# Suffix sums of a stick-breaking attention: fp32 matmuls replaced by fp32r matmuls on a high and a low part

## The chip, the cores and the metric

One core of one Trainium2 chip runs the whole program in one launch. The metric is the device time of a launch in microseconds (us). Below, TensorE is PE, ScalarE is ACT, VectorE is DVE, GpSimd is POOL, and SP issues the DMAs.

## The reference

The reference is a two-part model on a sequence of 256 positions, 1024 wide, in fp32: a block with a retention layer and a stick-breaking layer, each between two gated feed-forward layers and followed by a gated projection, and then a short convolution and a block attention. The change touches only the stick-breaking attention, with 8 heads of 128:

```python
def block(args):
    q_blk, b = args
    qpos = b * SB_BLOCK + jnp.arange(SB_BLOCK)
    z = jnp.einsum('bhqd,bhkd->bhqk', q_blk, k) * scale
    mask = (kpos[None, :] < qpos[:, None])[None, None]
    log_one_minus = jnp.where(mask, jax.nn.log_sigmoid(-z), 0.0)
    rem = lax.cumsum(log_one_minus, axis=3, reverse=True) - log_one_minus
    a = jnp.where(mask, jnp.exp(jax.nn.log_sigmoid(z) + rem), 0.0)
    return jnp.einsum('bhqk,bhkd->bhqd', a, v)
```

Around it stand `proj = h @ w_in` (1024 by 3072) and `o @ w_out` (1024 by 1024).

## The kernel before, in words

**The weight stream.** All weights of the model pass through the same pipeline, in slots numbered through the whole program. A slot is 256 rows by 512 columns of a weight. SP loads it into one of 4 `raw` buffers; ACT rounds it to fp32r as `w_hi` (`split` on ACT, L961); DVE makes `w_lo`, the rest that the rounding left (`split` on DVE, L1354); PE forms each product as three fp32r matmuls of 512 columns (hi by hi, hi by lo, lo by hi, L492 to L494, `products`). `w_hi` and `w_lo` are rings of 8 slots. SP reloads a raw buffer once `w_lo` of the slot four before is made.

**Orders written out by hand.** Each engine runs one program, in order. `split_to(n)` on ACT or on DVE means: make the parts of all slots below n that are not yet made. An instruction placed behind `split_to(n)` waits for all of them; and a `w_lo` on DVE waits for the `w_hi` of the same slot on ACT. PE works through the phases: `sb_in` (the projection, slots s0 to s0+23, in 12 groups, two groups for 4 slots, 24 matmuls each) and `sb_out` (slots s0+24 to s0+31). Between groups stand hooks with the attention's own work: after group 5 `sb_z` of heads 0 to 3 (the scores), after group 6 `sb_rem` of heads 0 and 1, after group 7 `sb_rem` of heads 2 and 3 and then `sb_mix` of heads 0 and 1 (weights by values), after group 8 `sb_mix` of heads 2 and 3; heads 4 to 7 have `sb_z` after group 10, `sb_rem` after step 1 of `sb_out` and `sb_mix` after step 3.

**One head.** PE writes z into a bank `turn[k]`. ACT makes log(1 + exp(-|z|)) in three steps (`sb_log`, L1181 to L1185). DVE adds max(z, 0) (L1638) and multiplies by the negated causal mask (L1642): the result `loss` is 384 columns wide, the three causal 128 by 128 blocks side by side. `sb_rem` then adds to the scores, in the same bank, the suffix sums of `loss`, by matmuls with a triangle of ones, with a block of ones, and with the identity on a tile of -1e30 outside the mask. All four are fp32 matmuls, and the trace shows each as two PE instructions (x16 for 8 heads). ACT then takes the exponential (`sb_exp`, L1191), and PE multiplies by the values. `sb_rows(m)` on ACT (L1162) copies the sums of group m out.

**The order on ACT** in this stretch: rows 4, flat, rows 5, `sb_log` 0 and 1, `split_to(s0+20)`, `sb_log` 2 and 3, rows 6, `sb_exp` 0 and 1, rows 7, `split_to(s0+24)`, and so on. Rows 7 wait for the sums of group 7. **On DVE**: `split_to(s0+16)`, `sb_loss` 0 and 1, `split_to(s0+20)`, `sb_loss` 2 and 3, `split_to(s0+24)`, the low parts of y for heads 0 to 3, `split_to(s0+28)`, `sb_loss` 4 to 7, `split_to(s0+32)`.

Of the kernel before, what the change touches and what calls it, by code (L numbers as in the profile page):

```python
# [23 lines left out]
F32 = mybir.dt.float32  # L24
F32R = mybir.dt.float32r
I32 = mybir.dt.int32
ACT = mybir.ActivationFunctionType
ALU = mybir.AluOpType
AX_X = mybir.AxisListType.X

P = 128
SEQ = 256
# [29 lines left out]
SW_QK, SW_V, SW_QT, SW_KT, SW_HEAD = 0, 1024, 2048, 3072, 4096  # L62
SW_MASK, SW_NEG, SW_TRI, SW_ONES = 7168, 7552, 7936, 8064
# [148 lines left out]
def build(nc, x, p_in, positions, norm_gains, ffn_w_gate, ffn_w_up, ffn_w_down, ret_w_in, ret_gn_gain,  # L212
          ret_w_out, sb_w_in, sb_w_out, ple_w_gate, ple_w_proj, norm_g_2, conv_w_in_2, conv_w_2,
          conv_w_out_2, attn_w_in_2, q_norm_g_2, k_norm_g_2, attn_w_out_2, consts, out):
    with ExitStack() as ctx:
        def sb(name, shape, dt=F32):
            return ctx.enter_context(nc.sbuf_tensor(name, shape, dt))

        def sem(name):
            return ctx.enter_context(nc.semaphore(name))  # L220
# [7 lines left out]
        y_hi = sb("y_hi", [P, FC, SEQ], F32R)  # L228
        y_lo = sb("y_lo", [P, FC, SEQ], F32R)
# [7 lines left out]
        ident = sb("ident", [P, P])  # L237
# [4 lines left out]
        work = sb("work", [P, WORK])  # L242

        sums = [ctx.enter_context(nc.psum_tensor(f"sums{i}", [P, COLS], F32)) for i in range(BANKS)]
        turn = [ctx.enter_context(nc.psum_tensor(f"turn{i}", [P, COLS], F32)) for i in range(4)]
# [24 lines left out]
        gn_loaded, decay_loaded, mask_loaded = sem("gn_loaded"), sem("decay_loaded"), sem("mask_loaded")  # L270
# [12 lines left out]
        mx = {n: sem("mx_" + n) for n in (  # L283
            "roped", "rope_step", "turned", "flat", "scores", "weights", "mixed", "stats", "gn_r",
            "gn_step", "gate", "y", "y_step")}
        sbs = {n: sem("sb_" + n) for n in ("turned", "flat", "z", "log", "act_step", "dve_step", "loss", "rem", "a", "o")}
        cv = {n: sem("cv_" + n) for n in ("mul", "turned", "flat", "step", "y", "pad")}
        mb = {n: sem("mb_" + n) for n in (
            "sq", "sq_step", "r", "normed", "turned", "flat", "s", "t", "max", "negmax", "exp",
# [17 lines left out]
        def lin(value, step, j):  # L307

            return value if j is None else j * step + value

        def wait_slot_free(eng, n, j=None):

            if n >= RING:
                kind, value = RELEASE[n - RING]
                if kind == "used":
                    eng.wait_ge(slot_used, lin(value, 6, j))
                else:
                    eng.wait_ge(sums_done, lin(value, 4, j))

        def mb_transposed(half):  # L320

            if half == 0:
                return work[:, MW_QT:MW_QT + 1024], work[:, MW_KT:MW_KT + 1024]
            rows = fg[:, :, :, :].rearrange("p t q n -> p (t q n)")
            return rows[:, 0:1024], rows[:, 1024:2048]
# [158 lines left out]
        def _(pe):  # L484
# [241 lines left out]
            def sb_rem(hd):  # L726

                k = hd % 4
                pe.wait_ge(sbs["loss"], hd + 1)
                loss = work[:, SW_HEAD + (hd % 4) * 768 + 384:SW_HEAD + (hd % 4) * 768 + 768]  # L730
                tri, ones = work[:, SW_TRI:SW_TRI + P], work[:, SW_ONES:SW_ONES + P]
                kw = dict(start=False, skip_group_check=True)
                pe.matmul(turn[k][:, 0:SEQ], tri, loss[:, 0:SEQ], stop=False, **kw)
                pe.matmul(turn[k][:, SEQ:384], tri, loss[:, SEQ:384], stop=False, **kw)
                pe.matmul(turn[k][:, P:SEQ], ones, loss[:, SEQ:384], stop=False, **kw)
                pe.matmul(turn[k][:, 0:384], ident[:, :], work[:, SW_NEG:SW_NEG + 384], stop=True, **kw).then_inc(sbs["rem"], 1)

            def sb_mix(hd):

# [207 lines left out]
        def _(act):  # L947
# [9 lines left out]
            def split(n, j=None):  # L957

                act.wait_ge(raw_loaded[n % RAW], lin(32 * (n // RAW + 1), 64, j))
                wait_slot_free(act, n, j)  # L960
                act.activation(w_hi[:, n % RING].rearrange("p c n -> p (c n)"),  # L961
                               raw[:, n % RAW].rearrange("p c n -> p (c n)"), ACT.Copy).then_inc(hi_made, 1)

            def split_to(n):
                while split_next[0] < min(n, SLOTS):
                    split(split_next[0])
                    split_next[0] += 1
# [184 lines left out]
            def sb_rows(m):  # L1152

                half, which, t = m // 6, (m % 6) // 2, m % 2
                if which < 2 and m >= 2:

                    act.wait_ge(sbs["turned"], 4 * half + 2 * which)
                if which == 2 and half:
                    act.wait_ge(sbs["o"], 4)
                at = (SW_QK if which < 2 else SW_V) + t * 512  # L1160
                act.wait_ge(sums_done, ph_sb.group0 + m + 1)
                act.activation(work[:, at:at + 512], sums[(ph_sb.group0 + m) % BANKS][:, :], ACT.Copy,  # L1162
                               scale=r_in[:, t:t + 1]).then_inc(act_read, 1)
# [3 lines left out]
            def sb_flat(which, half):  # L1167
                for i in range(2):
                    act.wait_ge(sbs["turned"], 4 * half + 2 * which + i + 1)
                    if half:  # L1170
                        act.wait_ge(sbs["z"], 4)
                    at = (SW_QT if which == 0 else SW_KT) + 512 * i
                    act.activation(work[:, at:at + 512], turn[2 * which + i][:, :], ACT.Copy,
                                   scale=(SDH ** -0.5 if which == 0 else 1.0)).then_inc(sbs["flat"], 1)

            def sb_log(hd):

                k = hd % 4
                at = work[:, SW_HEAD + k * 768:SW_HEAD + k * 768 + 384]
                act.wait_ge(sbs["z"], hd + 1)  # L1180
                act.activation(at, turn[k][:, 0:384], ACT.Abs).then_inc(sbs["act_step"], 1)  # L1181
                act.wait_ge(sbs["act_step"], 2 * hd + 1)
                act.activation(at, at, ACT.Exp, scale=-1.0).then_inc(sbs["act_step"], 1)
                act.wait_ge(sbs["act_step"], 2 * hd + 2)
                act.activation(at, at, ACT.Ln, bias=1.0).then_inc(sbs["log"], 1)  # L1185

            def sb_exp(hd):

                k = hd % 4
                act.wait_ge(sbs["rem"], hd + 1)  # L1190
                act.activation(work[:, SW_HEAD + k * 768:SW_HEAD + k * 768 + 384], turn[k][:, 0:384],  # L1191
                               ACT.Exp).then_inc(sbs["a"], 1)
# [5 lines left out]
            s0 = ph.slot0  # L1198
# [1 line left out]
            split_to(s0 + 12)  # L1200
            sb_rows(2); sb_flat(0, 0); sb_rows(3)
            split_to(s0 + 16)
            sb_rows(4); sb_flat(1, 0); sb_rows(5)
            act.preload_act_table_set("natural_log_exp_and_others")
            for hd in range(2):
                sb_log(hd)
            split_to(s0 + 20)
            for hd in range(2, 4):
                sb_log(hd)
            sb_rows(6)  # L1210
            sb_exp(0); sb_exp(1)
            sb_rows(7)
            split_to(s0 + 24)
# [8 lines left out]
            sb_log(4); sb_log(5)  # L1222
            sb_rows(11)
            sb_log(6); sb_log(7)
            split_to(s0 + 32)

            def sb_late():
                for hd in range(4, 8):
                    sb_exp(hd)
                for hd in range(4, 8):  # L1230
                    sb_y_hi(hd)
# [19 lines left out]
            for m in range(16):  # L1251
                half, i, t = m // 8, (m % 8) // 2, m % 2
# [3 lines left out]
                at = (CW_C, CW_X, CW_B, CW_Z)[i] + t * 512  # L1256
# [90 lines left out]
        def _(dve):  # L1347
# [10 lines left out]
            def split_to(n):  # L1358
                while split_next[0] < min(n, SLOTS):
                    split(split_next[0])  # L1360
                    split_next[0] += 1
# [269 lines left out]
            s0 = ph.slot0  # L1631

            def sb_loss(hd):

                k = hd % 4
                at = SW_HEAD + k * 768
                dve.wait_ge(sbs["log"], hd + 1)
                dve.scalar_tensor_tensor(out=work[:, at + 384:at + 768], in0=turn[k][:, 0:384], scalar=0.0,  # L1638
                                         in1=work[:, at:at + 384], op0=ALU.max, op1=ALU.add).then_inc(sbs["dve_step"], 1)
                dve.wait_ge(sbs["dve_step"], hd + 1)  # L1640
                dve.wait_ge(mask_loaded, 16)
                dve.tensor_tensor(work[:, at + 384:at + 768], work[:, at + 384:at + 768], work[:, SW_MASK:SW_MASK + 384],  # L1642
                                  ALU.mult).then_inc(sbs["loss"], 1)

            def sb_y_lo(hd):
                y_lo_of(turn[hd % 4][:, 0:SEQ], y_base("sb") + hd + 1, hd, 1)

            split_to(s0 + 16)
            sb_loss(0); sb_loss(1)
            split_to(s0 + 20)  # L1650
            sb_loss(2); sb_loss(3)
            split_to(s0 + 24)
            for hd in range(4):
                sb_y_lo(hd)
            split_to(s0 + 28)
            for hd in range(4, 8):
                sb_loss(hd)
            split_to(s0 + 32)

            plain_post("sb_out", 6, [lambda: [sb_y_lo(hd) for hd in range(4, 8)]])  # L1660

# [141 lines left out]
            s0 = ph.slot0  # L1803
# [48 lines left out]
```

## Time and profile before

| what | value |
|---|---|
| median of 3 runs | 1415.43 us (1415.26 to 1415.75) |
| profiled execution, its own time | 1416.9 us |
| its span in the trace | 1415.0 us |
| mean granted clock of PE | 0.997 |
| PE busy | 1386.2 us, 98% of the span |
| weight loads of PE (PEld) busy | 1140.1 us, 81% |
| DVE busy | 846.0 us, 60% |
| ACT busy | 728.4 us, 51% |

The profile is of one execution. Matmuls overlap in a pipeline, so the durations of single matmuls add up to more than the time they take; the distance between two starts is what one costs. A clock of 1.00 is TensorE's higher level of 2.4 GHz, 0.50 its lower level of 1.2 GHz. In a timeline, rows of the same kind that follow each other are merged, and a bracket gives the idle time before a row and what ended it.

### The profile page before, as it was taken

The page shows a single profiled execution, that of the slowest core. Times are in us where ns is not written, and L with a number is a line of the kernel's source. Part 1 is how long each engine was busy: PE and PEld are TensorE (multiplying, and loading weights), DVE is VectorE, ACT ScalarE, POOL GpSimd, SP SyncE. Part 2 cuts the span into 40 slices and gives each one's busy share as a digit, 9 for nine tenths or more (in the row PEclk, how much of TensorE's full clock was granted, in tenths as well). Part 3 has the DMA queues.
Part 4 walks back from the last instruction along what each step waited for, and adds up shares of the span by engine and source line. Part 5 has one row for each costly group of instructions (what it writes and reads, how often), then busy time and mean ns, then how long its engine had stood idle before and what let it go on. Part 6 is the DMA issues. An engine that isn't in the chain of part 4 may idle for free. (4 is left out here: it accounts for less than half of the span.)

```text
span 1415.0 us, 18949 instructions
## 1 busy us (share of the span) xinstructions
PE 1386.2 (98%) x6434; PEld 1140.1 (81%) x6434; DVE 846.0 (60%) x1066; ACT 728.4 (51%) x1026; POOL 62.1 (4%) x117
## 2 busy tenths in 40 slices
PE   6999999999999999999999999999999999999998
PEld 5888888888888888878888888878888878888776
DVE  5555666676665555575555544575555676676664
ACT  5444455444454444474444456554444565555683
POOL 0000000000010000010000000010000010002000
PEclk9999999999999999999999999999999999999998
DMA  7656555555646566446567453455666456545431
GB/s 228 188 186 210 174 175 187 182 190 188 206 135 194 188 207 222 148 150 210 178 201 233 160 179 134 134 164 178 189 212 230 143 174 203 181 151 171 151 114 60
DMA packets 186237, 251.41 MB, mean 178 GB/s; under 512 B 15508, under 2 KB 115388, under 8 KB 186172
## 3 DMA queue, kind: packets, MB, share of 16 engines
q1 hardware_dynamic: 186172, 250.56, 54.9%
q8 instruction: 39, 0.64, 0.2%
q14 instruction: 26, 0.21, 0.1%
HBM read 249.45 MB, written 1.05 MB: 177 GB/s over the span
## 5 line engine op out<-in xcount | busy, mean ns | idle before, releaser
L1354 DVE TENSOR_TENSOR w_lo<-raw,w_hi 128x1024 fp32r<-128x1024 f32 x460 | 540.0, 1221 | 179.9 <-ACT w_hi L961 178.6
L492 PE MATMUL sums<-w_hi,x_hi 128*128 128x512 f32 x1312 | 522.0, 398 | 10.9 <-DVE w_lo L1354 6.1
L961 ACT ACTIVATE w_hi<-raw 128x1024 fp32r<-128x1024 f32 x460 | 460.6, 1051 | 130.6 <-PE sums L494 69.0
L494 PE MATMUL sums<-w_hi,x_lo 128*128 128x512 f32 x1312 | 512.7, 391 | 0.0
L493 PE MATMUL sums<-w_lo,x_hi 128*128 128x512 f32 x1312 | 511.7, 390 | 0.0
L492 PEld LDWEIGHTS sums<-w_hi,x_hi 128*128 128x128 f32 x1312 | 247.0, 188 | 65.9 <-issue 16.0
L494 PEld LDWEIGHTS sums<-w_hi,x_lo 128*128 128x128 f32 x1312 | 246.6, 188 | 52.3
L493 PEld LDWEIGHTS sums<-w_lo,x_hi 128*128 128x128 f32 x1312 | 247.2, 188 | 49.7 <-issue 1.0
L492 PE MATMUL sums<-w_hi,y_hi 128*128 128x512 f32 x512 | 202.2, 395 | 0.0
L493 PE MATMUL sums<-w_lo,y_hi 128*128 128x512 f32 x512 | 200.2, 391 | 0.0
L494 PE MATMUL sums<-w_hi,y_lo 128*128 128x512 f32 x512 | 200.1, 391 | 0.0
L1024 ACT ACTIVATE work<-sums,stat 128x256 f32<-128x256 f32 x88 | 41.7, 474 | 240.6 <-PE sums L494 240.5
L1430 DVE SCALAR_TENSOR_TENSOR work<-sums,stat,work 128x256 f32<-128x256 f32 x88 | 42.5, 483 | 180.5 <-ACT work L1024 180.5
L494 PEld LDWEIGHTS sums<-w_hi,y_lo 128*128 128x128 f32 x512 | 96.7, 189 | 20.4
L493 PEld LDWEIGHTS sums<-w_lo,y_hi 128*128 128x128 f32 x512 | 96.7, 189 | 19.6
L492 PEld LDWEIGHTS sums<-w_hi,y_hi 128*128 128x128 f32 x512 | 96.7, 189 | 19.6
L1008 ACT ACTIVATE work<-sums,stat 128x512 f32<-128x512 f32 x54 | 37.1, 687 | 132.2 <-PE sums L494 131.0
L973 ACT ACTIVATE x_hi<-xg 128x512 fp32r<-128x512 f32 x40 | 24.6, 631 | 58.2 <-DVE xg L1368 58.1
L906 POOL TENSOR_TENSOR stat<-stat,neg_half 128x1 f32<-128x1 f32 (+1 forms) x48 | 42.7, 889 | 4.0
L920 POOL TENSOR_TENSOR stat<-stat 128x1 f32<-128x1 f32 x16 | 3.6, 223 | 847.7 <-ACT junk L985 823.9
L1384 DVE TENSOR_TENSOR fg<-sums,post_gain 128x512 f32<-128x512 f32 x24 | 16.6, 692 | 36.8 <-ACT junk L985 36.7
L903 POOL TENSOR_SCALAR stat<-stat 128x1 f32<-128x1 f32 (+1 forms) x48 | 15.5, 323 | 402.3 <-ACT junk L977 236.2
(169 smaller groups left out, 766.0 us busy)
## 6 DMA issues: line engine op xcount, KB each, us to landing
raw<-in_ffn_w_gate_dram SPq DMA_DIRECT2D x176, 256.0 KB, 3.9
raw<-in_ffn_w_up_dram SPq DMA_DIRECT2D x176, 256.0 KB, 4.8
raw<-in_ffn_w_down_dram SPq DMA_DIRECT2D x176, 256.0 KB, 3.7
raw<-in_ret_w_in_dram SPq DMA_DIRECT2D x96, 256.0 KB, 4.2
raw<-in_conv_w_in_dram SPq DMA_DIRECT2D x64, 256.0 KB, 4.0
raw<-in_attn_w_in_dram SPq DMA_DIRECT2D x64, 256.0 KB, 3.9
raw<-in_sb_w_in_dram SPq DMA_DIRECT2D x48, 256.0 KB, 3.6
raw<-in_ret_w_out_dram SPq DMA_DIRECT2D x32, 256.0 KB, 4.1
```

The lines of the kernel that those rows point to most:

```text
L492: pe.matmul(bank[:, :], a, wh, start=(first and c == 0), stop=False, skip_group_check=True)
L493: pe.matmul(bank[:, :], a, wl, start=False, stop=False, skip_group_check=True)
L494: mm = pe.matmul(bank[:, :], b, wh, start=False, stop=(last and c == SC - 1), skip_group_check=True)
L903: pool.tensor_scalar(tmp, src, scale, eps, ALU.mult, ALU.add).then_inc(pool_step, 1)
L906: pool.tensor_tensor(dst, tmp, neg_half[:, 0:k], ALU.pow).then_inc(sign, 1)
L961: act.activation(w_hi[:, n % RING].rearrange("p c n -> p (c n)"), raw[:, n % RAW].rearrange("p c n -> p (c n)"), ACT.Copy).then_inc(hi_mad ...
L973: act.activation(x_hi[:, 4 * q:4 * q + 4, t * P:(t + 1) * P], xg[:, q, :].rearrange("p (c t) -> p c t", c=4), ACT.Copy).then_inc(x_hi_made, 1)
L1008: act.activation(dst, sums[(ph.group0 + m) % BANKS][:, :], func, **kw).then_inc(act_read, 1)
L1024: act.activation(work[:, t * FB:(t + 1) * FB], sums[(ph.group0 + m) % BANKS][:, 0:FB], ACT.Silu, scale=r_in[:, t:t + 1]).then_inc(act_read, 1)
L1354: dve.tensor_tensor(w_lo[:, n % RING].rearrange("p c n -> p (c n)"), raw[:, n % RAW].rearrange("p c n -> p (c n)"), w_hi[:, n % RING].rear ...
L1384: dve.tensor_tensor(fg[:, t, n, :], sums[(ph.group0 + 2 * t + n) % BANKS][:, :], post_gain[:, n * COLS:(n + 1) * COLS], ALU.mult).then_inc ...
L1430: dve.scalar_tensor_tensor(out=work[:, HW_HID + t * FB:HW_HID + (t + 1) * FB], in0=sums[(ph.group0 + m) % BANKS][:, FB:2 * FB], scalar=r_i ...
```

## The change

The suffix sums are formed by fp32r matmuls. `loss` is split, as the weights are, into an fp32r high part (a copy on ACT, `sb_loss_hi`) and a low part (a subtraction on DVE, `sb_loss_lo`); both are kept in columns of `y_hi` and `y_lo` that this stage doesn't use. The constant tiles (the -1e30 tile, triangle, ones, identity) are rounded once to fp32r on ACT (`sb_masks`). A head now has five matmuls: identity by the -1e30 tile, triangle by high and by low (384 columns each), ones by high and by low (128 columns each). Calls are added to the written orders of ACT and DVE, and `split_to` calls with new bounds stand ahead of some of them. No DMA is added. The core of the diff:

```diff
             def sb_rem(hd):
 
                 k = hd % 4
-                pe.wait_ge(sbs["loss"], hd + 1)
-                loss = work[:, SW_HEAD + (hd % 4) * 768 + 384:SW_HEAD + (hd % 4) * 768 + 768]
-                tri, ones = work[:, SW_TRI:SW_TRI + P], work[:, SW_ONES:SW_ONES + P]
+                pe.wait_ge(sbs["masks"], 2)
+                pe.wait_ge(sbs["loss_lo"], hd + 1)
+                high, low = sb_loss_parts(hd)
                 kw = dict(start=False, skip_group_check=True)
-                pe.matmul(turn[k][:, 0:SEQ], tri, loss[:, 0:SEQ], stop=False, **kw)
-                pe.matmul(turn[k][:, SEQ:384], tri, loss[:, SEQ:384], stop=False, **kw)
-                pe.matmul(turn[k][:, P:SEQ], ones, loss[:, SEQ:384], stop=False, **kw)
-                pe.matmul(turn[k][:, 0:384], ident[:, :], work[:, SW_NEG:SW_NEG + 384], stop=True, **kw).then_inc(sbs["rem"], 1)
+                pe.matmul(turn[k][:, 0:384], sb_eye, sb_neg, stop=False, **kw)
+                pe.matmul(turn[k][:, 0:384], sb_tri, high, stop=False, **kw)
+                pe.matmul(turn[k][:, 0:384], sb_tri, low, stop=False, **kw)
+                pe.matmul(turn[k][:, P:SEQ], sb_ones, high[:, SEQ:384], stop=False, **kw)
+                pe.matmul(turn[k][:, P:SEQ], sb_ones, low[:, SEQ:384], stop=True, **kw).then_inc(sbs["rem"], 1)
...
+            def sb_masks():
+
+                act.wait_ge(mask_loaded, 16)
+                act.activation(y_hi[:, :, :].rearrange("p c t -> p (c t)")[:, 16 * SEQ:16 * SEQ + 640],
+                               work[:, SW_NEG:SW_NEG + 640], ACT.Copy).then_inc(sbs["masks"], 1)
+                act.activation(sb_eye, ident[:, :], ACT.Copy).then_inc(sbs["masks"], 1)
+
+            def sb_loss_hi(hd):
+
+                at = SW_HEAD + (hd % 4) * 768 + 384
+                act.wait_ge(sbs["loss"], hd + 1)
+                if hd >= 4:
+                    act.wait_ge(sbs["rem"], hd - 3)
+                act.activation(sb_loss_parts(hd)[0], work[:, at:at + 384], ACT.Copy).then_inc(sbs["loss_hi"], 1)
...
             split_to(s0 + 16)
-            sb_rows(4); sb_flat(1, 0); sb_rows(5)
+            sb_rows(4); sb_flat(1, 0); sb_masks(); sb_rows(5)
             act.preload_act_table_set("natural_log_exp_and_others")
             for hd in range(2):
                 sb_log(hd)
+            split_to(s0 + 18)
+            sb_loss_hi(0); sb_loss_hi(1)
             split_to(s0 + 20)
             for hd in range(2, 4):
                 sb_log(hd)
             sb_rows(6)
+            sb_loss_hi(2); sb_loss_hi(3)
             sb_exp(0); sb_exp(1)
             sb_rows(7)
             split_to(s0 + 24)
...
             sb_log(6); sb_log(7)
+            split_to(s0 + 30)
+            sb_loss_hi(4); sb_loss_hi(5)
             split_to(s0 + 32)
+            sb_loss_hi(6); sb_loss_hi(7)
...
+            def sb_loss_lo(hd):
+
+                at = SW_HEAD + (hd % 4) * 768 + 384
+                high, low = sb_loss_parts(hd)
+                dve.wait_ge(sbs["loss_hi"], hd + 1)
+                dve.tensor_tensor(low, work[:, at:at + 384], high.bitcast(F32), ALU.subtract).then_inc(sbs["loss_lo"], 1)
...
             split_to(s0 + 16)
             sb_loss(0); sb_loss(1)
+            split_to(s0 + 18)
+            sb_loss_lo(0); sb_loss_lo(1)
             split_to(s0 + 20)
             sb_loss(2); sb_loss(3)
+            split_to(s0 + 21)
+            sb_loss_lo(2); sb_loss_lo(3)
             split_to(s0 + 24)
             for hd in range(4):
                 sb_y_lo(hd)
             split_to(s0 + 28)
             for hd in range(4, 8):
                 sb_loss(hd)
+            split_to(s0 + 30)
+            sb_loss_lo(4); sb_loss_lo(5)
             split_to(s0 + 32)
+            sb_loss_lo(6); sb_loss_lo(7)
```

## Rows read from the trace of the kernel before

**Rows 1.** The page: busy time of PE; then its line of the granted clock.
```profile
PE 1386.2 (98%) x6434; PEld 1140.1 (81%) x6434; DVE 846.0 (60%) x1066; ACT 728.4 (51%) x1026; POOL 62.1 (4%) x117
...
PEclk9999999999999999999999999999999999999998
```

**Rows 2.** Windows, one stretch: span, busy of PE, PEld, DVE, ACT, POOL, clock, DMA.
```profile
820.00:950.00 130.00, 128.40 (x617) 106.23 (x616) 68.99 (x82) 75.96 (x118) 5.18 (x11) 1.00 0.49 160
```

**Rows 3.** Timeline of PE at its three hooks: start us, length us, then the instruction.
```profile
854.57 0.60 PE L733 MATMUL turn<-work 128*128 128x256 f32 x2
855.01 0.38 PE L734 MATMUL turn<-work 128*128 128x128 f32 x2
855.45 0.81 PE L736 MATMUL turn<-work,ident 128*128 128x384 f32 x2
856.10 0.59 PE L733 MATMUL turn<-work 128*128 128x256 f32 x2
...
857.85 0.39 PE L493 MATMUL sums<-w_lo,x_hi 128*128 128x512 f32 x1
858.08 0.39 PE L494 MATMUL sums<-w_hi,x_lo 128*128 128x512 f32 x1
...
863.08 0.60 PE L733 MATMUL turn<-work 128*128 128x256 f32 x2
...
866.13 0.59 PE L744 MATMUL turn<-work 128*128 128x256 f32 x2
...
901.60 0.60 PE L733 MATMUL turn<-work 128*128 128x256 f32 x2
...
907.93 0.39 PE L493 MATMUL sums<-w_lo,y_hi 128*128 128x512 f32 x1
```

**Rows 4.** Timeline of ACT around the same hooks.
```profile
846.69 0.69 ACT L1162 ACTIVATE work<-sums,stat 128x512 f32<-128x512 f32 x1 [4.69 <-PE sums L494]
...
851.70 3.88 ACT L961 ACTIVATE w_hi<-raw 128x1024 fp32r<-128x1024 f32 x4
...
863.34 0.69 ACT L1162 ACTIVATE work<-sums,stat 128x512 f32<-128x512 f32 x1 [3.45 <-PE sums L494]
863.92 3.89 ACT L961 ACTIVATE w_hi<-raw 128x1024 fp32r<-128x1024 f32 x4
```

**Rows 5.** Timeline of DVE around the same hooks.
```profile
852.41 0.56 DVE L1642 TENSOR_TENSOR work<-work 128x384 f32<-128x384 f32 x1
852.89 4.62 DVE L1354 TENSOR_TENSOR w_lo<-raw,w_hi 128x1024 fp32r<-128x1024 f32 x4
857.43 0.55 DVE L1638 SCALAR_TENSOR_TENSOR work<-turn,work 128x384 f32<-128x384 f32 x1
...
865.00 4.63 DVE L1354 TENSOR_TENSOR w_lo<-raw,w_hi 128x1024 fp32r<-128x1024 f32 x4 [5.26 <-ACT w_hi L961]
...
901.20 4.62 DVE L1354 TENSOR_TENSOR w_lo<-raw,w_hi 128x1024 fp32r<-128x1024 f32 x4
```

**Rows 6.** Timelines late in the run: PE, PE, DVE, then PE again.
```profile
1325.08 0.47 PE L492 MATMUL sums<-w_hi,x_hi 128*128 128x512 f32 x1 [0.87 <-DVE w_lo L1354]
1325.39 0.40 PE L493 MATMUL sums<-w_lo,x_hi 128*128 128x512 f32 x1
```
```profile
1380.80 0.69 DVE L1574 TENSOR_TENSOR y_lo<-turn,y_hi 128x512 fp32r<-128x512 f32 x1 [1.07 <-ACT y_hi L1308]
```
```profile
1381.64 0.87 PE L837 MATMUL turn<-ident,work 128*128 128x128 f32 x3 [3.43 <-DVE y_lo L1574]
```

**Rows 7.** Windows around PE's longest idle time after the start; columns as in rows 2.
```profile
1379.50:1380.00 0.50, 0.00 (x0) 0.00 (x0) 0.23 (x1) 0.49 (x2) 0.00 (x0) 1.00 0.62 82
1380.00:1380.25 0.25, 0.00 (x0) 0.00 (x0) 0.00 (x0) 0.25 (x2) 0.00 (x0) 0.83 0.80 262
1380.16:1387.00 6.84, 5.36 (x14) 4.33 (x15) 3.94 (x13) 4.50 (x14) 0.00 (x0) 0.50 0.43 142
1387.00:1387.50 0.50, 0.50 (x5) 0.40 (x4) 0.00 (x0) 0.50 (x3) 0.00 (x0) 1.00 0.00 0
```

More of the change, by code:

```diff
@@ L285, in build @@
             "gn_step", "gate", "y", "y_step")}
-        sbs = {n: sem("sb_" + n) for n in ("turned", "flat", "z", "log", "act_step", "dve_step", "loss", "rem", "a", "o")}
+        sbs = {n: sem("sb_" + n) for n in ("turned", "flat", "z", "log", "act_step", "dve_step", "loss", "loss_hi", "loss_lo",
+                                           "masks", "rem", "a", "o")}
         cv = {n: sem("cv_" + n) for n in ("mul", "turned", "flat", "step", "y", "pad")}
@@ L318, in wait_slot_free, with sb_loss_parts @@
                     eng.wait_ge(sums_done, lin(value, 4, j))
+        def sb_loss_parts(hd):
+            at = 8 * SEQ + (hd % 4) * 384
+            return [a[:, :, :].rearrange("p c t -> p (c t)")[:, at:at + 384] for a in (y_hi, y_lo)]
+        sb_neg, sb_tri, sb_ones, sb_eye = [y_hi[:, :, :].rearrange("p c t -> p (c t)")[:, 16 * SEQ + lo:16 * SEQ + hi]
+                                           for lo, hi in ((0, 384), (384, 512), (512, 640), (640, 768))]
         def mb_transposed(half):
```

## Prediction

> **What bounds the kernel now.** I read the page first: PE is busy 98% of the span, at the full clock in nearly every slice [rows 1]. Then the windows over the stick-breaking stage: PE 128.4 of 130 us, ACT 76 and DVE 69, clock 1.00 [rows 2]. So PE is the bound, in this stage too, and the other two have room on the average. An average doesn't say whether a given result is there when PE asks for it, so next I read the timelines of PE, ACT and DVE side by side at the three places where `sb_rem` stands [rows 3 to 5]. The reader should see that PE doesn't wait for `loss` there now: at the first hook `loss` of head 1 is done at 852.97 (852.41 + 0.56, rows 5) and PE begins at 854.57 [rows 3]. Since PE has almost no gaps, any stall of PE in front of a hook goes one for one into the time, and any PE work saved comes out of it.
>
> **What PE saves.** A head costs 856.10 - 854.57 = 1.53 us now [rows 3]: 896 columns, each passed twice; the two matmuls of 128 columns, four passes, take 855.45 - 855.01 = 0.44, 0.11 a pass. An fp32r matmul of 512 columns costs 858.08 - 857.85 = 0.23 (0.227 over the 23 from 857.85 to 863.08), or 0.443 ns a column [rows 3]. The three of 384 columns should cost 3 x 0.170 = 0.51. The two of 128 columns have no row. Below, streaming alone would be 0.057 each; above, no fp32r matmul in the trace costs more than the 0.227 of four times the width. I take 0.11, what a 128-column pass with its own weight load costs in rows 3, since here too each has a weight load. So a head costs r = 0.51 + 0.22 = 0.73 us, between 0.62 and 0.96. If `sb_loss_lo` were always in time, the change would save 8 x (1.53 - 0.73) = 6.4 us.
>
> The Trainium skill's page "TensorE: Matmul & The Clock Gate", section "Back-to-back issue gap", gives an isolated gap of N/2.4 + 2.5 ns, 56 ns at 128 columns; the rows show 227 ns where it gives 216 at 512, and 110 for an fp32 pass of 128. By an estimate from that page, r would be 0.60 and my sum below, which holds 6 r, would be lower by 0.8 us.
>
> **What ACT and DVE add.** ACT gets 8 copies of 384 columns and two copies of constants. A copy of 1024 columns costs 3.88/4 = 0.97 [rows 4]; I take 0.44 for 384 columns (between 0.36, in proportion, and 0.5), 4.5 us in all with the constants. The constants are made in the 4.69 us for which ACT is idle ahead of its copy at 846.69 [rows 4]; without that cover they would cost 1.0. DVE gets 8 subtractions: 4.62/4 = 1.155 us for 1024 columns [rows 5]; the loss operations of 384 columns last 0.56 and the next begins 852.89 - 852.41 = 0.48 later [rows 5]. I take 0.48 of DVE's time and 0.55 until the result is seen, together 3.9 us. Neither engine is the bound, so as work this is free. What counts is where they stand in the queues. SP gets no DMA, and is moved past nothing; the `w_lo` of slots behind the subtractions come about 1 us later, and with them the reloads of raw buffers, whose `w_hi` are due many microseconds on. I cost that at nothing.
>
> From DVE's result to PE's start I take 0.15 (1381.64 - 1381.49, rows 6), and 0.09 more for a restart (0.31 instead of 0.227 between two products after a wait, rows 6).
>
> **Hook after group 6, heads 0 and 1.** `sb_loss_lo(0)` stands behind `w_lo` of s0+16 and s0+17: 852.89 + 2 x 1.155 = 855.20, done at 855.75. Its high part is there: ACT makes `w_hi` of those two from 851.70 to 853.64, and then the copy, before 854.2 [rows 4]. PE would start at 855.90 instead of 854.57, and leave at 855.90 + 2 r + 0.09 = 857.45. Before, it left at 857.62 (857.85 - 0.227, rows 3). **Gain 0.2 us** instead of 1.6. What is late next: `w_lo` of s0+18 and s0+19 and then `sb_loss(2)`, which begins at about 858.45 instead of 857.43, `sb_loss(3)` ends near 860.8, and its high part is there by 861.3. That is ahead of the next hook at 862.9.
>
> **Hook after group 7, heads 2 and 3.** This is the main term. `sb_loss_lo(2)` stands behind `split_to(s0+21)`, which is `w_lo` of s0+20. That needs `w_hi` of s0+20 from ACT, and on ACT this stands behind rows 7, which wait for the end of group 7 on PE. In the rows: PE ends group 7 at 863.08 [rows 3]; rows 7 begin at 863.34, `w_hi` at 863.92 [rows 4], `w_lo` at 865.00 [rows 5]; it takes 1.155, and `sb_loss_lo(2)` ends at 866.70. PE, which stands at this very hook from 863.08, can only start at 866.85: an idle time of 3.8 us that the new wait creates. Behind it in PE's queue are `sb_rem`, `sb_mix` of two heads and group 8. Before, the two heads took 866.13 - 863.08 = 3.05 [rows 3]. Now 3.77 + 2 r + 0.09 = 5.32. **Loss 2.3 us.** That the hook comes 0.2 earlier changes nothing, as the whole chain hangs on PE's own group 7.
>
> **Hook in `sb_out`, heads 4 to 7.** DVE begins `w_lo` of s0+28 at 901.20 [rows 5], right behind `sb_loss(7)`; the new order is two slots, `sb_loss_lo` 4 and 5, two slots, `sb_loss_lo` 6 and 7. So `sb_loss_lo(4)` begins at 903.51, `sb_loss_lo(6)` at 901.20 + 4 x 1.155 + 2 x 0.48 = 906.78, done at 907.33. PE, at the hook from 901.60 [rows 3], starts heads 4 and 5 at 904.2, is done with them near 905.8, starts head 6 at 907.48 and leaves at 907.48 + 2 r + 0.09 = 909.03. Before it left at 907.70 (907.93 - 0.227, rows 3). **Loss 1.3 us.** The exponentials and `sb_mix` come 5 us later and keep their cover.
>
> Queues together: -0.2 + 2.3 + 1.3 = **+3.4 us** (as a formula, 6 r - 1.0).
>
> **The clock.** After the idle time of 3.43 us at 1378.2 [rows 6] PE's granted clock fell from 1.00 to 0.50, at 1380.16, some 2 us into the idle time, and stayed at the lower level (1.2 GHz) to 1387.0; PE worked 5.36 us of that at half speed [rows 7]. That cost about 2.7 us. Light work (small matmuls) stood ahead of that gap, dense products stand ahead of this one; on the other hand the new gap of 3.8 us is longer, and two more gaps (2.6 and 1.7 us) stand close together at the third hook. I expect one fall. If it comes as late in the gap as in the row, 6.84 - (3.8 - 2.0) = 5.0 us of work run at half speed: **+2.5 us**. The Trainium skill has a rule against this change here (same page, section "Why this matters for your kernels": PE-idle gaps between bursts of matmuls bring the lower clock back); the trace agrees in rows 7.
>
> Sum: 3.4 + 2.5 = +5.9 us. The profiled execution has 1416.9 us (its span 1415.0 and 1.9 around it), 1.5 above the median of the runs, so it becomes 1422.8, and the median 1415.43 + 5.9 = **1421.3 us**.
>
> **Rivals.**
> - Stalls as above, clock stays up: 1415.4 + 3.4 = 1418.8 (1418.1 with r at 0.62, 1420.2 with 0.96). For it: dense work on both sides, and after the gap of 0.87 us the products run 0.23 apart [rows 6], which is the higher level. Chance 0.24.
> - The clock falls at both places, or 128-column fp32r matmuls are dear as well: 3.4 + 2 x 2.5 = +8.4, 1423.8. Chance 0.18.
> - Faster: the subtractions are ready when PE comes, and PE saves what it can, 6.4 us at most: 1409. It is decided at the second hook: with `w_hi` of s0+20 made over 3.8 us earlier, ahead of rows 7, the loss of 2.3 turns into 1.6 gained. The written order speaks against it; a gain would need me to have misread it. Chance 0.06.
> - The stalls are there but shorter, with cheap small matmuls, so that the sum is within 0.2% (2.8 us, about what a measurement of this kernel can tell from no change): near 1417.5. Chance 0.08.
> - The change not doing what it says (fp32r still passed twice, r about 1.4): 6 x 1.4 - 1.0 = +7.4, 1422.8 without a fall. Chance 0.04.
>
> **How the numbers follow.** The forecast has 0.40. The range, 1417.8 to 1424.3, takes in the stall alone with r at its lower end and the double fall, and leaves out the gain, most of the small cases and the end where all goes wrong. Slower by over 0.2%: 0.40 + 0.18 + 0.04, and of the 0.24 some 0.18 (it lies below the bound only if r is under 0.64), 0.80. Faster 0.06. The rest, 0.14, is the same.
>
> **What would show it.** In the profile after: an idle time of PE of 3.7 to 3.9 us ahead of the identity matmul of head 2, ended by DVE's low part; one of 1.3 at head 0, of 2.6 at head 4 and 1.7 at head 6; the starts of two heads in a row 0.73 us apart; a stretch of some microseconds at clock 0.50 behind the second hook; ACT and DVE each 4 us busier. It would be wrong above all if the clock doesn't fall, by 2.5 us, and entirely if the low parts of heads 2 and 3 are not held by rows 7.

## The result, and the profile after

| | before | after |
|---|---|---|
| median | 1415.59 us (1415.26 to 1416.25, 4 runs) | 1424.22 us (1422.52 to 1425.32, 4 runs) |
| profiled execution, its span | 1415.0 us | 1420.3 us |
| mean granted clock in the span | 0.997 | 0.994 (0.992 in the other three runs) |
| PE busy | 1386.2 us | 1384.2 us |

The ratio is 1.006 (95% interval 1.0045 to 1.0074): 8.6 us slower. The forecast was 1421.3 in a range of 1417.8 to 1424.3, so the direction is right and the time lies just inside the upper end. The profiled execution of after (1422.52 us) is its fastest one, that of before (1416.9 us) slower than all its timed ones.

The page and the stretch of the stage, which answer to [rows 1, 2]:

```profile
PE 1384.2 (97%) x6410; PEld 1139.4 (80%) x6410; DVE 849.5 (60%) x1074; ACT 733.5 (52%) x1036; POOL 61.8 (4%) x117
...
PEclk9999999999999999999999999999999999999998
```
```profile
820.00:950.00 130.00, 120.36 (x560) 100.39 (x559) 66.61 (x85) 77.34 (x123) 4.80 (x10) 0.96 0.44 145
```

Over the whole run PE is busy for 2 us less, and nothing looks amiss there. In the stretch, though, PE is busy for 120.4 of 130 us instead of 128.4, and the clock is 0.96 instead of 1.00. The line of the clock on the page of the profile, in tenths, doesn't show it. The timeline of PE at the three hooks, against [rows 3]:

```profile
852.72 0.39 PE L503 MATMUL sums<-w_hi,x_lo 128*128 128x512 f32 x1
854.24 0.41 PE L742 MATMUL turn<-y_hi 128*128 128x384 f32 x1 [1.13 <-DVE y_lo L1681]
854.49 0.34 PE L743 MATMUL turn<-y_hi 128*128 128x384 f32 x1
854.67 0.34 PE L744 MATMUL turn<-y_lo,y_hi 128*128 128x384 f32 x1
854.84 0.22 PE L745 MATMUL turn<-y_hi 128*128 128x128 f32 x1
854.90 0.27 PE L746 MATMUL turn<-y_lo,y_hi 128*128 128x128 f32 x1
855.01 0.39 PE L742 MATMUL turn<-y_hi 128*128 128x384 f32 x1
...
861.06 0.39 PE L503 MATMUL sums<-w_hi,x_lo 128*128 128x512 f32 x1
865.05 0.41 PE L742 MATMUL turn<-y_hi 128*128 128x384 f32 x1 [3.60 <-DVE y_lo L1681]
...
906.29 0.41 PE L742 MATMUL turn<-y_hi 128*128 128x384 f32 x1 [2.40 <-DVE y_lo L1681]
...
909.50 0.66 PE L742 MATMUL turn<-y_hi 128*128 128x384 f32 x1 [0.92 <-DVE y_lo L1681]
```

All four idle times are ended by DVE's low part, at the places that the prediction names. The fourth, 0.92 us ahead of head 6, is shorter than the 1.7 that were named. The starts also show what a head costs: 855.01 - 854.24 = 0.77 us right behind a wait instead of 1.53; the first 128-column matmul is followed by the next after 0.06, the second by the next head's after 0.11. The chain behind the longest wait stands in the timelines of ACT and then of DVE, against [rows 4, 5]:

```profile
861.55 0.69 ACT L1172 ACTIVATE work<-sums,stat 128x512 f32<-128x512 f32 x1 [1.27 <-PE sums L503]
862.13 3.89 ACT L971 ACTIVATE w_hi<-raw 128x1024 fp32r<-128x1024 f32 x4
```
```profile
863.21 1.23 DVE L1385 TENSOR_TENSOR w_lo<-raw,w_hi 128x1024 fp32r<-128x1024 f32 x1 [4.25 <-ACT w_hi L971]
864.36 1.02 DVE L1681 TENSOR_TENSOR y_lo<-work,y_hi 128x384 fp32r<-128x384 f32 x2
```

The copy of rows 7 waits for PE's group 7, the high part of slot s0+20 for that copy, its low part for that, and only then comes the low part of head 2's loss, which has been computable since about 859. Note DVE: it was idle for 4.25 us just before, with the subtraction next but one in its queue. The windows of the clock, against [rows 7], show the two falls, the short windows on either side of the second one, and the part of it behind the wait for head 6:

```profile
866.17:869.58 3.41, 3.41 (x14) 3.05 (x13) 3.03 (x4) 1.21 (x3) 0.00 (x0) 0.50 0.80 275
907.00:907.13 0.13, 0.13 (x4) 0.13 (x3) 0.13 (x1) 0.13 (x1) 0.00 (x0) 0.99 1.11 394
907.13:913.95 6.82, 5.90 (x20) 5.45 (x20) 3.83 (x5) 3.34 (x7) 0.00 (x0) 0.50 0.92 289
909.50:913.95 4.45, 4.45 (x14) 4.16 (x15) 1.46 (x2) 1.44 (x4) 0.00 (x0) 0.50 0.99 317
913.95:914.10 0.15, 0.15 (x2) 0.11 (x2) 0.00 (x0) 0.00 (x0) 0.00 (x0) 0.98 0.96 314
```

The clock falls to its lower level 1.1 us after the 3.60 us of idle time ends, and again 0.8 us after the 2.40 us end. PE works 3.41 + 5.90 = 9.3 us at half speed, but not all of it costs time. Heads 4 and 5 are slowed ahead of the wait for head 6, which ends when DVE's low part is there; so the wait gets shorter instead (0.92 us for 1.7). What no wait takes up is 3.41 us at the second hook and 4.45 us behind the start of head 6: half of each, 1.7 and 2.2 us, should be the price.

**Where the time went.** Executions differ outside the stage: its first scores come at 844.9 to 846.5 us in all profiles, and 498.9 to 499.9 us lie behind its last matmul. So I compare the time between the same two instructions, from the first scores of head 0 (at 846.49 before, 844.88 after) to the start of the last mix instruction of 256 columns, which is read to 0.1 us.

| us | before | after |
|---|---|---|
| scores of head 0 to scores of head 4 (first and second hook) | 41.59 | 45.34 |
| scores of head 4 to last mix (third hook) | 27.22 | 30.58 |
| sum | 68.81 | 75.92 (+7.1) |

### The profile page after: what moved, and what is told of

Read it like the earlier page. It is cut to its first block and busy times, and to the rows that moved or that the text cites. A ratio compares the mean times of both kernels' runs of the same rounds, so it can differ in the third digit from the quotient of the medians.

```text
span 1420.3 us, 18931 instructions
## 1 busy us (share of the span) xinstructions
PE 1384.2 (97%) x6410; PEld 1139.4 (80%) x6410; DVE 849.5 (60%) x1074; ACT 733.5 (52%) x1036; POOL 61.8 (4%) x117
```

## The experiments

Each is compared with the kernel before in runs on the same chip, and ratios are of these. The chips differ between experiments, so where two experiments are compared, each is taken from its own before (medians 1415.59, 1415.69 and 1415.82), or their stages are; "stage" is the sum of that table. The interval of a ratio reaches 1.3 to 2.4 us to either side.

**Is the added work itself the cost?** The fp32 matmuls of before, waiting for `loss`; the constants and parts are still made in their new places, and no one waits for them.

```diff
                 pe.wait_ge(sbs["masks"], 2)
-                pe.wait_ge(sbs["loss_lo"], hd + 1)
-                high, low = sb_loss_parts(hd)
+                pe.wait_ge(sbs["loss"], hd + 1)
+                loss = work[:, SW_HEAD + (hd % 4) * 768 + 384:SW_HEAD + (hd % 4) * 768 + 768]
...
-                pe.matmul(turn[k][:, 0:384], sb_tri, high, stop=False, **kw)
-                pe.matmul(turn[k][:, 0:384], sb_tri, low, stop=False, **kw)
...
+                pe.matmul(turn[k][:, 0:SEQ], tri, loss[:, 0:SEQ], stop=False, **kw)
+                pe.matmul(turn[k][:, SEQ:384], tri, loss[:, SEQ:384], stop=False, **kw)
```

> The changed kernel with the four fp32 matmuls of before, waiting for loss as before; the constants, the high and the low parts are still made in their places, but nobody waits for the low parts. Theory (the added work is hidden): 1415.6, within 0.7 us of before. Rival (the added 4.5 us on ACT and 3.9 on DVE delay something): 1417 to 1424.

Measured: 1416.0 us, ratio 1.0005 (0.9996 to 1.0014), stage 68.83 against 68.81. ACT is busy for 4.5 us more than before and DVE for 3.7 in its profile, and that work is hidden.

**The second hook alone mended.**

```diff
-            split_to(s0 + 21)
             sb_loss_lo(2); sb_loss_lo(3)
```

> The changed kernel without the call split_to(s0+21) on DVE, so that the low parts of heads 2 and 3 no longer stand behind w_lo of slot s0+20. Theory (queue position and the clock fall that the idle time brings): at the second hook PE loses 3.9 us against before in the trace of the changed kernel and would gain 1.6 instead, so 5.5 us less than the changed kernel's 1424.2, 1418.7 (1418 to 1419.7); no idle time of PE there and clock 1.00 until the third hook, where the fall remains. Rival (the extra copies and subtractions, or the new matmuls, are what costs): no change, 1424.

Measured: 1418.26 us, 1.0017 (1.0008 to 1.0026), 6.0 us less than after. From head 0's to head 4's scores 39.88 instead of 45.34, so 5.5 less, as expected. Removing one call, which only sets the place of work that is done anyway, gives back two thirds of the loss. The third hook kept its idle time and the fall behind it.

**All three hooks mended.** The same instructions, in another order: the parts of heads 0 and 1 stand around the first weight slot, those of 2 and 3 behind their loss, those of 4 and 5 ahead of rows 11, those of 6 and 7 around slot s0+28.

```diff
@@ ACT
-            split_to(s0 + 18)
-            sb_loss_hi(0); sb_loss_hi(1)
+            sb_loss_hi(0)
+            split_to(s0 + 17)
+            sb_loss_hi(1)
...
             sb_log(4); sb_log(5)
+            sb_loss_hi(4); sb_loss_hi(5)
             sb_rows(11)
             sb_log(6); sb_log(7)
-            split_to(s0 + 30)
-            sb_loss_hi(4); sb_loss_hi(5)
+            sb_loss_hi(6)
+            split_to(s0 + 29)
+            sb_loss_hi(7)
             split_to(s0 + 32)
-            sb_loss_hi(6); sb_loss_hi(7)
@@ DVE
-            split_to(s0 + 18)
-            sb_loss_lo(0); sb_loss_lo(1)
+            sb_loss_lo(0)
+            split_to(s0 + 17)
+            sb_loss_lo(1)
...
-            split_to(s0 + 21)
             sb_loss_lo(2); sb_loss_lo(3)
...
-            for hd in range(4, 8):
-                sb_loss(hd)
-            split_to(s0 + 30)
-            sb_loss_lo(4); sb_loss_lo(5)
+            sb_loss(4); sb_loss(5)
+            sb_loss_lo(4); sb_loss_lo(5)
+            sb_loss(6); sb_loss(7)
+            sb_loss_lo(6)
+            split_to(s0 + 29)
+            sb_loss_lo(7)
             split_to(s0 + 32)
-            sb_loss_lo(6); sb_loss_lo(7)
```

> All high and low parts moved ahead of the weight slots at the three hooks (one slot is left between two of them at the first and the third). Same matmuls and same extra work as in the changed kernel. Theory: PE waits at no hook, a head costs 0.77 us instead of 1.53, and 8 x 0.76 = 6.1 us come off before: 1409.5 (1408.8 to 1410.5), clock 1.00 through the stage. Rival (the work added to ACT and DVE costs time by itself, or the fp32r matmuls save nothing): 1415 or more.

Measured: 1410.67 us, 0.9962 (0.9948 to 0.9975): 4.9 us faster than before, 13.6 faster than the change as made. Stage 62.69, 6.1 less than before. The median lies just above the expected range (1408.8 to 1410.5): 1.2 us less came off than in the stage. The times of executions of this version spread over 2.2 us, and I can't place the rest. The windows and the timeline of PE:

```profile
820.00:950.00 130.00, 128.40 (x621) 107.66 (x620) 75.59 (x94) 84.23 (x133) 5.11 (x11) 1.00 0.52 166
```
```profile
861.46 0.33 PE L742 MATMUL turn<-y_hi 128*128 128x384 f32 x1
861.63 0.34 PE L743 MATMUL turn<-y_hi 128*128 128x384 f32 x1
861.81 0.34 PE L744 MATMUL turn<-y_lo,y_hi 128*128 128x384 f32 x1
861.98 0.23 PE L745 MATMUL turn<-y_hi 128*128 128x128 f32 x1
862.04 0.28 PE L746 MATMUL turn<-y_lo,y_hi 128*128 128x128 f32 x1
862.16 0.38 PE L742 MATMUL turn<-y_hi 128*128 128x384 f32 x1
...
862.90 0.64 PE L754 MATMUL turn<-work 128*128 128x256 f32 x2
```

No bracket stands at the second hook any more, the clock is 1.00, and two heads take 862.90 - 861.46 = 1.44 us instead of 3.05.

**One wait at a time.** From the mended version, the second hook alone was put back, and then the third alone.

```diff
+            split_to(s0 + 21)
             sb_loss_lo(2); sb_loss_lo(3)
```

> The version with all parts moved ahead (1410.7), but with split_to(s0+21) on DVE back in its place, so that the second hook alone waits as in the changed kernel. Theory: this one call costs what the second hook lost, 3.8 us of idle time and a fall of the clock of 1.7 to 2.5, less nothing: 1410.7 + 5.5 to 6.3 = 1416.2 to 1417, with the clock at 0.50 for 3 to 6 us behind it. Rival (the three hooks' losses don't add, for instance because a later wait takes up an earlier one): under 1415.

Measured: 1416.24 us, 1.0004 (0.9995 to 1.0013). That is 0.4 us above its before, where the mended version is 4.9 below, so the call costs 5.3 us. From head 0's to head 4's scores it is 43.95 instead of 38.48 us, 5.5 more. One misplaced call is enough to eat the whole gain.

The third hook's diff is the part of the diff above from `sb_log(4)` on ACT and from the loop over heads 4 to 7 on DVE, taken back.

> The version with all parts moved ahead, but with the third hook in the order of the changed kernel. Theory: the third hook alone costs what it lost in the changed kernel against the version with all moved: 24.2 to 30.6 us from the scores of head 4 to the last mix, 6.4 with its fall of the clock (4.3 without), so 1410.5 + 6.4 = 1416.9 (1414.8 to 1417.5). Rival (the losses don't add up): under 1414.

Measured: 1417.48 us, 1.0011 (1.0002 to 1.0021), 1.8 above its before and so 6.7 above the mended version; its part of the stage 31.10 instead of 24.21, 6.9 us. The first hook's wait costs 1.4 in the traces: from head 0's to head 4's scores 39.88 us with the second hook alone mended and 38.48 with the first mended too. In the stages the three make 5.5 + 6.9 + 1.4 = 13.8 us, and the change as made lost 75.92 - 62.69 = 13.2. In the medians the last two hooks make 12 of 13.6, which leaves about 1.5 for the first. The losses add, to half a microsecond in the stages; the medians can't tell so finely.

**How much is the clock?** The order of the change is kept, and PE does work of no use while it waits, in a part of the bank that nothing reads. It waits for `loss` first, since DVE reads that bank until then.

```diff
                 pe.wait_ge(sbs["masks"], 2)
+                pe.wait_ge(sbs["loss"], hd + 1)
+                for _ in range({2: 15, 4: 10, 6: 6}.get(hd, 0)):
+                    pe.matmul(turn[k][:, 384:512], ident[:, :], ident[:, :], start=False, stop=False, skip_group_check=True)
                 pe.wait_ge(sbs["loss_lo"], hd + 1)
```

> The changed kernel with its order untouched, but PE does 128-column matmuls of no use, into columns of the bank that nothing reads, before it waits for the low parts of heads 2 (15 of them, 3.3 us), 4 (10, 2.2 us) and 6 (6, 1.3 us). The waits end as late as before, only PE isn't idle in them. Theory (more than half of the loss is the clock): no fall of the clock at these hooks, and the time is before plus 3.4 us of stalls, 1419.0 (1418.3 to 1420), against 1424.2 of the changed kernel. Rival (the clock doesn't follow from the idle time, or its fall costs nothing): 1424.

Measured: 1419.52 us, 1.0027 (1.0016 to 1.0037). Stage 72.15, which is 3.34 us above before. The timeline of PE and the windows of the two hooks:

```profile
862.07 3.51 PE L741 MATMUL turn<-ident 128*128 128x128 f32 x30
865.74 0.44 PE L745 MATMUL turn<-y_hi 128*128 128x384 f32 x1 [0.17 <-DVE y_lo L1684]
```
```profile
860.00:875.00 15.00, 14.84 (x87) 13.11 (x86) 6.23 (x8) 7.21 (x12) 0.00 (x0) 1.00 0.60 206
900.00:915.00 15.00, 14.81 (x88) 13.07 (x87) 9.63 (x13) 9.49 (x16) 0.00 (x0) 1.00 0.54 175
```

From the end of group 7 (last start plus 0.23) to the start of head 2 PE takes 3.7 us, as in the change (3.8); PE is just not idle in it, and the clock stays at its higher level. The stage splits well: 75.92 - 72.15 = 3.8 us are the clock, 1.7 of it up to head 4's scores (45.34 against 43.65) and 2.1 behind (30.58 against 28.50), which are the 1.7 and 2.2 us worked out above from the windows. The other 3.3 us are the stalls less what the matmuls save. In the medians this version is 3.7 us above its before and the change 8.6, so filling the idle time gives back 4.9.

**Do the falls always come at the same instructions?** The changed kernel once more.

> The changed kernel itself, profiled once more. Theory: the stalls last as long as in the first profile (1.1, 3.6, 2.4 us of idle time ahead of heads 0, 2 and 4), while the falls of the clock begin and end at other points of the stage, so the time from the first scores to the last mix is again 72.2 (the stalls alone) plus 2 to 6 us. Rival (the falls are tied to the instructions): again at 866.2 to 869.6 and 907.3 to 913.5 relative to the same instructions, 75.9 us.

Measured: 1424.53 us, 1.0064 (1.0047 to 1.0081), stage 76.16. Idle times 1.13, 3.60 and 2.40 us as the first time. The fall behind the second hook came 1.4 us after PE resumed (867.17 - 865.74) instead of 1.1, the one at the third hook 1.1 (908.13 - 907.01) instead of 0.8. They were as long as the first time:

```profile
867.17:870.58 3.41, 3.41 (x13) 2.96 (x12) 2.64 (x4) 1.25 (x4) 0.00 (x0) 0.50 0.77 266
908.13:914.96 6.83, 5.66 (x20) 5.11 (x19) 3.54 (x5) 3.05 (x6) 0.00 (x0) 0.50 0.95 288
```

So the stalls repeat, the falls keep their length, and their starts move by some tenths of a microsecond. In both profiles the stage has two. A stage of 76.2 us fits both forecasts; only the starts tell them apart, and they side with the theory, by little. The runs without a profile are slower by 0.5 to 2.8 us than the profiled ones, at a mean clock of 0.992 instead of 0.994. A mean lower by 0.002 over 1422 us is 2.8 us of lost clock (1.4 to 4.3, as the means are rounded), so longer or further falls would explain it; these runs leave no trace, and where they fall stays open.

**Is a fall of the clock always lost time?** The prediction took its price from the fall late in the kernel before [rows 6, 7]. There PE got 15 matmuls of no use, in a free bank, ahead of the wait of 3.43 us.

```diff
+                if hd == 13:
+                    out_ph = PHASES["moba_out"]
+                    wait_bank(out_ph, 0)
+                    for _ in range(15):
+                        pe.matmul(sums[out_ph.group0 % BANKS][:, 0:P], ident[:, :], ident[:, :], start=False, stop=False,
+                                  skip_group_check=True)
                 if hd in (13, 15):
                     pe.wait_ge(y_lo_made, y_base("moba") + (1 if hd == 13 else 2))
```

> The kernel before, with 15 matmuls of no use (3.3 us, into a bank that is free) ahead of PE's wait of 3.43 us late in the block attention, after which its trace has the clock at 0.50 for 6.8 us. Theory (the idle time brings the fall, and half speed over 5.4 us of work costs 2.7 us): the clock stays at 1.00 and the time is 1415.6 - 2.7 = 1412.9 (1412.3 to 1414). Rival (the fall comes from the light work ahead of the gap, or the matmuls of no use delay the wait's end): 1415.6 or more.

Measured: 1415.78 us, 1.0000 (0.9991 to 1.0009). The theory (1412.9) failed in half: the clock does stay up (1.00 in the window below, mean 0.999 or 1.0 in all 11 runs), but the time shows no gain. Windows, then the timeline of PE:

```profile
1377.00:1387.00 10.00, 9.13 (x67) 8.13 (x65) 5.77 (x15) 7.63 (x18) 0.00 (x0) 1.00 0.33 107
```
```profile
1380.66 0.55 PE L843 MATMUL turn<-ident,work 128*128 128x128 f32 x3
...
1387.99 0.52 PE L843 MATMUL turn<-ident,work 128*128 128x128 f32 x3 [1.86 <-DVE y_lo L1580]
```

Counted from the turn of head 13, PE now ends the products behind it some 2.5 us earlier, and it stands for 1.86 us at the next wait of the same kind, for head 15. DVE's part for that head, which waits for ACT, starts 6.5 us after that turn, against 6.9 before, so it hangs little on PE's speed. From the turn of head 13 to the products behind that of head 15 PE takes 7.6 us instead of 8.0. The late fall was covered by a later wait, all but some 0.4 us, which the medians can't show. The same matmuls in the mended version:

> The version with all parts moved ahead (1410.7) together with the 15 matmuls of no use ahead of the late wait. Theory (the two don't touch each other): 1410.7 - 2.7 = 1408.0 (1407.3 to 1409.2). Rival: as the version without them, 1410.7.

Measured: 1410.26 us, 0.9963 (0.995 to 0.9977), nothing over the mended version's 0.9962. The rival is right here too.

## Why the prediction was right, and where it was off

- **What PE saves.** r was put at 0.73; measured 0.77 right behind a wait and 0.75 for the next head (855.01 to 855.76), and 0.72 a head in the mended version. The stage of the mended version is 6.1 us shorter where 8 x (1.53 - 0.73) = 6.4 was named. The estimate by the Trainium skill's page "TensorE: Matmul & The Clock Gate" (section "Back-to-back issue gap"), 0.60, was further off, although the spacing of 0.06 between the two small matmuls is close to its 56 ns. The pair takes 0.17, and after it the first of a head takes 0.22 to 0.23 instead of 0.17. Loads of weights start at least 0.11 apart there, so they may set this pace; no run tests that.
- **What ACT and DVE add.** Hidden, as said: stage 68.83 against 68.81 with the added work and the old matmuls.
- **First hook.** Predicted a gain of 0.2, where no wait would give 1.6. From the end of group 6 to the first product of group 7 PE took 3.05 before and takes 2.86 after (852.95 to 855.81, ends taken as the last start plus 0.227): 0.19. The 1.4 us by which the wait spoils the gain are those measured above.
- **Second and third hook, without the clock.** Predicted +2.3 and +1.3, with the first hook +3.4 in all. With the idle times filled the stage was 3.3 us longer: 2.1 up to head 4's scores (43.65 against 41.59), where -0.2 + 2.3 was forecast, and 1.3 behind (28.50 against 27.22). The reason given, that the low parts of heads 2 and 3 are held by rows 7, is shown by taking the call out (-6.0 us) and by putting it back alone (+5.3).
- **The clock.** This is the term that was mis-sized. "I expect one fall" failed: both profiles have two in the stage, at the second and the third hook, as in the rival "the clock falls at both places" (1423.8, chance 0.18). The price of each, 2.5, was too high: they cost 1.7 and 2.1 us, 3.8 together. The prediction let the fall come inside the idle time and last 6.84 us less what was left of it, 5.0. At the second hook it came 1.1 us after PE had resumed and lasted 3.41 us; at the third it lasted 6.82, of which the wait for head 6 took up the first 2.4. That one term too few and one price too high partly cancel is luck.
- **The rest.** Two falls for 3.8 instead of one for 2.5 make 1.3 of the 2.9 us by which 1421.3 fell short of 1424.2. The other 1.6 us are not in the traces of the stage, which is 7.1 to 7.4 us longer where the medians differ by 8.6 to 8.8. They are mostly in the runs that leave no trace, and their cause stays open. That the profiled execution of after has 1422.5 us where 1422.8 was named is luck too: its stage came 1.6 us earlier than in the profile of before.
- **The price's source.** "That cost about 2.7 us" of the late fall in before was read off the work done at half speed, without asking what is late next. It cost some 0.4 us at its place, and nothing that the medians show. The same reading holds at the second hook of the change, since PE sets the pace behind it (half of 3.41 us, 1.7 measured), and at the third only for the part behind the wait for head 6.

## What to carry to other kernels

When work is split off to another engine, its place in that engine's queue counts, and not its length: here 8 to 9 us of added work cost nothing, while one call placed a slot too late cost over 5. Before such a result is waited for, follow every instruction ahead of it in its queue back to its own inputs; if one of them comes from the engine that waits, the wait holds at least that whole loop. And a stall of the engine that is the bound costs more than its length, if the clock falls behind it; but a fall costs only where no later wait takes it up, so price it at its place.

## What the runs showed of the hardware that was not expected

- The clock fell after PE had already resumed: 1.1 and 1.4 us after the end of 3.60 us of idle time in the two profiles of the change (0.6 with the second hook alone put back), 0.8 and 1.1 us after the end of 2.40 us. Late in the kernel before it fell 2 us into an idle time. A gap can thus be paid for although PE is at work again when the fall comes.
- The falls in the stage had one of two lengths: 3.41 us at the second hook in all three profiles that have one there, 6.82 or 6.83 us at the third in all four. The late fall lasted 6.83 us in the kernel before and 3.41 in the run with the idle times filled. The idle time of 1.13 us at the first hook brought none.
- Small fp32 matmuls of no use (128 columns, 0.22 us each, identity by identity) kept the clock at 1.00 through the same waits.
- An fp32r matmul of 384 columns costs 0.17 to 0.18 us in a stream (0.25 right after a wait, 0.22 to 0.23 after the 128-column pair), and one of 128 columns 0.06, or 0.11 where a matmul with other weights follows. An fp32 matmul is two passes of 0.32 and of 0.11 for the same widths.
